# Transposing the running sums of the state space part once, and spreading each head's row with one product

## The reference, cut to what matters

```python
dt = softplus(dt_raw + dt_bias)                     # [tokens, heads]
a = -exp(a_log)
cum = cumsum(dt * a, axis=tokens)                   # [256, 32]
seg = cum[t, head] - cum[s, head]
decay_ts = exp(where(t >= s, seg, -inf))
w = (c_t . b_s) * decay_ts * dt_s
y[t] = sum over s of w[t, s] * x[s]                 # per head
```

## Time and profile before

| what | us |
|---|---|
| median of the runs (3) | 1957.97 |
| profiled execution, own time | 1953.04 |
| its span | 1951.2 |
| TensorE busy (PE) | 1786.4, 92% |
| VectorE busy (DVE) | 857.6, 44% |
| ScalarE busy (ACT) | 560.4, 29% |
| GpSimd busy (POOL) | 307.3, 16% |

### The profile page before, as it was taken

How to read it: one execution, slowest core, us unless ns; L and a number is a source line. 1 busy time by engine, 2 the same in 40 slices (tenths; PEclk the granted TensorE clock), 3 DMA queues, 4 the chain that set the end, 5 groups by cost and what they waited for, 6 DMA issues and landing times.

```text
span 1951.2 us, 32338 instructions
## 1 busy us (share of the span) xinstructions
PE 1786.4 (92%) x13254; PEld 1686.9 (86%) x13254; DVE 857.6 (44%) x2226; ACT 560.4 (29%) x1542; POOL 307.3 (16%) x284
## 2 busy tenths in 40 slices
PE   3999999999999878877899999997999999999998
PEld 2888887888889877777899899987999999899998
DVE  6631474333155677766968655333341113311010
ACT  1011224440033444434556432322322101321000
POOL 0100000000012544544334333230000000000000
PEclk9998999999999999999999999999999999999999
DMA  9952332133449999999999999996686687458883
GB/s 386 367 194 87 130 130 102 72 108 129 151 160 414 415 421 420 420 420 420 404 421 406 420 420 420 421 420 259 225 302 215 218 281 256 151 189 287 292 291 130
DMA packets 82658, 554.89 MB, mean 284 GB/s; under 512 B 8736, under 2 KB 15440, under 8 KB 15824
## 3 DMA queue, kind: packets, MB, share of 16 engines
q1 hardware_dynamic: 41088, 256.60, 36.2%
q0 software_dynamic: 39168, 285.23, 35.5%
q10 hardware_dynamic: 2256, 11.00, 1.4%
HBM read 551.72 MB, written 1.07 MB: 283 GB/s over the span
## 4 chain that ended last, share of the span: by engine, by line
PE 72%; DMA 17%; DVE 4%; ACT 3%; issue 3%; POOL 1%; ACTq 0%; DVEq 0%; POOLq 0%
PE PS L834 30%; PE PS L602 21%; PE PS L798 10%; DMA AUX<-in_peer_uv_dram,SCR 10%; DMA V<-in_peer_uv_dram,SCR 4%; DMA CONV<-in_peer_uv_dram,SCR 2%; PE PS L624 2%; PE PS L649 1%; DMA PROJ<-in_ada_dram 1%; DVE PROJ L1900 1%; PE PS L869 1%; PE PS L739 1%; PE PS L974 1%; PE PS L973 1%; PE PS L995 1%
## 5 line engine op out<-in xcount | busy, mean ns | idle before, releaser
L602 PE MATMUL PS<-H,ring 128*128 128x256 f32 x1408 | 314.9, 385 | 4.8 <-DVE H L1824 3.6
L602 PEld LDWEIGHTS PS<-H,ring 128*128 128x128 f32 x1408 | 270.3, 193 | 42.5 <-issue 4.3
L798 PE MATMUL PS<-PROJ,AUX 128*128 128x128 f32 x2048 | 254.3, 284 | 45.2 <-ACT PROJ L1283 45.0
L798 PEld LDWEIGHTS PS<-PROJ,AUX 128*128 128x128 f32 x2048 | 244.4, 199 | 52.7 <-ACT PROJ L1283 52.5
L834 PE MATMUL PS<-H,ring 128*128 128x128 f32 x2112 | 246.0, 275 | 0.0
L834 PEld LDWEIGHTS PS<-H,ring 128*128 128x128 f32 x2112 | 241.2, 192 | 1.0 <-issue 0.6
L1117 POOL DMA_INDIRECT AUX<-in_peer_uv_dram,SCR x128 | 145.5, 1137 | 552.7 <-DVE SCR L1884 314.2
L1900 DVE CUSTOM_DVE_ANT_0 PROJ<-AUX,PROJ 128x1024 f32<-128x1024 f32 x128 | 156.0, 1224 | 156.3 <-DMA AUX<-in_peer_uv_dram,SCR 155.9
L798 PE MATMUL PS<-PROJ,CONV 128*128 128x128 f32 x1536 | 187.6, 282 | 36.7 <-ACT PROJ L1283 36.7
L798 PEld LDWEIGHTS PS<-PROJ,CONV 128*128 128x128 f32 x1536 | 180.8, 197 | 41.6 <-ACT PROJ L1283 41.6
L834 PE MATMUL PS<-PROJ,ring 128*128 128x128 f32 x1632 | 187.9, 275 | 0.0
(11 more groups left out here) (299 smaller groups left out, 1772.4 us busy)
## 6 DMA issues: line engine op xcount, KB each, us to landing
ring<-in_stream_dram SPq DMA_DIRECT2D x181, 1024.0 KB, 4.9
AUX<-in_stream_dram SPq DMA_DIRECT2D x58, 1024.0 KB, 4.8
AUX<-in_ada_dram POOLq DMA_DIRECT2D x16, 1024.0 KB, 10.4
AUX<-in_ada_dram ACTq DMA_DIRECT2D x4, 1024.0 KB, 12.1
PROJ<-in_ada_dram ACTq DMA_DIRECT2D x4, 1024.0 KB, 21.0
AUX<-in_peer_uv_dram,SCR POOLq DMA_INDIRECT x128, 14.7
CONV<-bias_by_distance SPq DMA_DIRECT2D x1, 2048.0 KB, 12.6
CONV<-in_peer_uv_dram,SCR POOLq DMA_INDIRECT x96, 14.5
```

The lines of the kernel that those rows point to most:

```text
L602: mm = pe.matmul(acc(n, c), w[:, k, c * P:(c + 1) * P], src[:, g * DC + k, :], start=(g == 0 and k == 0 and (c == 0 or groups == 1)), stop ...
L798: mm = pe.matmul(y_chunk(t, c), UV[b][:, D + c * P:D + (c + 1) * P], DIAG[n % ND], start=(k == 0 and c % 4 == 0), stop=(k == SPT - 1), ski ...
```

## The change

A new job "ct" is put at h = 5: TensorE transposes `cum` (two transposes of 128 tokens by 32 heads) and VectorE copies the [32, 256] result to CUMT, on 32 partitions of `dts`, in the place of the four temporary fields. `cum_row(h)` then is one product: its stationary operand is column h of a 32 by 32 unit matrix, spread to 128 columns, its moving operand is CUMT.

```diff
@@ plan_jobs
         if h == 4:
             jobs += ["cum0", "cum1"]
+        if h == 5:
+            jobs.append("ct")
         if h:
             jobs.append(("yn", h - 1))
@@ program
         dt_, dtA, cum, dtx, dty, dtz, arow = (dts[:, i] for i in range(7))
+        CUMT = dts[0:32, 3:7].rearrange("p a t n -> p (a t n)")
@@ TensorE, loop over heads
+                if h == 5:
+                    o = open_bank(pe, "ct")
+                    for t in range(TT):
+                        wait_taken(pe, f"cum{t}")
+                        mm = pe.transpose(o[0:32, t * P:(t + 1) * P], cum[:, t, :], ident)
+                    made(mm, "ct")
                 if h:
                     norm_sum(h - 1)
@@ TensorE, cum_row
             def cum_row(h):
                 o = open_bank(pe, ("cr", h))
-                pe.matmul(o[:, 0:TOK], dtA[:, 0, h:h + 1].broadcast_to([P, P]), cst("triu"), start=True, stop=False)
-                made(pe.matmul(o[:, P:TOK], dtA[:, 1, h:h + 1].broadcast_to([P, P]), cst("triu", 0, P),
-                               start=False, stop=True), ("cr", h))
-
+                made(pe.matmul(o[:, 0:TOK], ident[0:32, h:h + 1].broadcast_to([32, P]), CUMT, start=True, stop=True), ("cr", h))
+
+            wait_taken(pe, "ct")
             for h in range(4):
                 cum_row(h)
@@ VectorE, loop over heads, behind head_var(h - 1)
+                if h == 5:
+                    wait_made(dve, "ct")
+                    taken(dve.tensor_copy(CUMT, bank("ct")[0:32, 0:TOK]), "ct")
```

## The result

The changed kernel takes 1965.79 us (median of 5, 1963.47 to 1969.34) against 1957.97 us: ratio 1.0041, 95% interval 1.0023 to 1.0059. A second set gave 1.0039 (1.0023 to 1.0054). By the means it is slower by 7.5 us in the first set and 7.6 us in the second; 0.8 us was forecast, too little to be told from nothing, and the time lies 4.2 us above the top of the range.

A forecast was written before the change was run, and what follows sets the result against it. TensorE, 72% of the chain, was taken to bound the kernel, with ScalarE and VectorE setting some places. Gains -3.3, changes of shape +1.4 and head 5 +2.7 gave +0.8 us: 1958.8 us, 8-in-10 range 1954.9 to 1961.6.

The forecast's parts named there:

- Gains from shorter rows: TensorE's rows, one product each: 0.22 us saved per head, 7.0 in all, of which 3.32 on the path.
- The rows in the middle of a block and behind the last `g` tile: Rows 10, 11, 14, 15, 18, 19, 22, 23 and 26 to 31: no gain, ScalarE and VectorE set the time.
- Changes of shape: Seven new changes on the path between 32-partition rows and full products: 0.2 us each, 1.4 us in all.
- The term of 0.6: Two transposes at head 5 with a change of shape in and out: 0.6 us, between 0.2 and 0.9.
- The wait at head 5: Second half of the scores waits for VectorE's copy behind a reciprocal: 2.7 us with the transposes, bounds 2.2 and 3.1.
- Sum of work: Whole kernel: gains -3.3, changes of shape +1.4 and head 5 +2.7 make +0.8 us.
- the rival "TensorE's clock falls": Heads 26 to 31, attention projection pays: +3.7 us, 1961.7; with a second fall at head 5, 1964.6; chance 0.08.
- the prediction's own last sign: TensorE's granted clock: the prediction fails if it leaves 1.00.
- cover for rows 4 and 5: Before the first `y` product TensorE idles 1.57 us for VectorE, so shortening rows 4 and 5 gives nothing.
- the idle 2.02 us at head 4 has 1.00: Argument against the clock falling: the stretch with that idle time at head 4 ran at 2.4 GHz throughout.
- fill a quarter of the array: Argument for the clock falling: heads 26 to 31 idle TensorE 0.22 us more each, rows using 32 of 128 partitions.

The follow-up runs named there:

- e3_rows_128: The change with VectorE's copy of the transposed sums ahead of head_var(4) and rows contracting over 128 partitions, not 32: -0.8 +- 2.0 us against before.
- e2: The change with VectorE's copy of the transposed sums moved ahead of head_var(4), rows still on 32 partitions: +4.1 +- 2.8 us against before.
- e1_ct_only: The change with the old two-product cum_row put back, keeping the transposes, copy and wait at head 5: +2.7 +- 2.5 us against before.
- e6: The change with its wait at head 5 kept, but rows contracting over all 128 partitions: +1.5 +- 2.0 us against before.
- e4_before_again: The kernel before, unedited, run again as a control with its own profile: -0.1 +- 1.9 us against before.
- e8_both_copies_first: e3_rows_128 with VectorE at head 4 also copying cum0 and cum1 ahead of head_var(3): -8.1 +- 2.2 us against before, ratio 0.9963, median 1949.99 us.
- e9: The kernel before with one edit, VectorE at head 4 copying cum0 and cum1 ahead of head_var(3): -1.0 +- 2.0 us against before.

## Why the prediction was wrong, point by point

**Gains from shorter rows: right.** From the last `cb` product to `g` tile 2 it is 2.84 us before, 2.23 in the profile after and 1.95 in e3_rows_128, where the full 0.88 show. Blocks are 11.40 us, 11.20 in e3. The rows in the middle of a block and behind the last `g` tile give nothing, as said: from `g` tile 7 to `attn` it is 18.34 us after and 18.23 before.

**Changes of shape: right for 32 partitions**, 0.2 us each: 11.40 against 11.20 for one, and for the two around rows 0 to 3 0.28 before tile 2 and 0.10 within it. **Wrong for the transposes:** with 32 columns between products of 128 they cost 0.22 us for both and nothing more (275.22 to 275.44 to the next product's normal start; head 5 in e2 is 2.69 against 2.47 us). The term of 0.6 was 0.2.

**The wait at head 5: right in place and making**, 2.5 us with the transposes where 2.7 stood; e1_ct_only has +2.7 +- 2.5, and taking the wait away saved 3.5 +- 3.9 (32 partitions) and 2.3 +- 3.0 us (128), which fits but is not clear of noise.

**Sum of work:** with these sizes -3.3 + 1.4 + 2.5 = +0.6 us. The measured change is 7.5. So the sum was sound and 7 us lay outside it. That the forecast's +0.8 is so near to +0.6 is in part luck: the transposes were put 0.4 too high and their wait 0.2 too low.

**The failed step is the rival "TensorE's clock falls", held at 0.08.** The sum of the forecast put the clock at nothing, and the prediction's own last sign, the granted clock leaving 1.00, is what came. The rival had one price, one place and one argument against it, and all three were off. The place: I put it at heads 26 to 31 and `attn`, where TensorE is least filled to the eye; there the clock stayed at 1.00 in the change's profile. It fell at pairs 0 and 1, where TensorE idles for ScalarE and VectorE (1.37 and 1.57 us before) and does thin work between, and where the earlier trace rows had shown that idle time to me as good news, cover for rows 4 and 5. The price: 2.9 us from one fall at head 2; here 5.5 in the stretch (85.96 us where the work gives 81.88 - 2.44 + 1.0 = 80.44), all but some 1.0 of it from the form on 32 partitions, and 1.7 in the profile behind head 5 (3.4 us at half the clock). 0.6 + 5.5 + 1.7 = 7.8, near the 7.5 measured. The runs bear out the 5.5 better than the 1.7: e1 and e6 lie 2.7 and 2.3 us above their partners, what the wait costs by work alone. The argument: "the idle 2.02 us at head 4 has 1.00" was one draw. In seven of eleven profiles the clock does fall behind that wait. The sentence that its rows "fill a quarter of the array" was the right lead; with 64 of 128 partitions the fall is short (one profile), with 32 it is long.

The Trainium skill, page "TensorE: Matmul & The Clock Gate", section "Part 1: The HAM clock gate", says that the gate follows how busy the array has been, and that how many slow matmuls one gets varies from run to run. The traces agree with the second: e4_before_again has falls at places where the first profile of before has none. They agree with the first in so far as the fall at the pairs begins in or right behind an idle time of 1.8 us on TensorE. e2 against e3 adds that after rows on 32 partitions the low clock lasts longer than after rows with as many columns on 128.

**Open.** Why e8_both_copies_first lies 8.1 us below before and not the 3 to 4 that its work allows (2.0 for head 4, 3.1 for rows without changes of shape, less 1 to 2 for the falls at the pairs); e3 and e9 alone have -0.8 and -1.0, and e8's mean granted clock, 0.9784, is hardly above the 0.9768 of before beside it. The falls that its profile lacks behind head 4 may be some of it, but e9 lacks them too. What it is in a product on 32 partitions that holds the clock less was not taken further; e3's weights are zero beyond one partition too, so it isn't how many of them are zero, but the data that stream through the other 96 partitions were not told apart from the number of partitions. The intervals against before are 2 to 3 us to a side, and each kernel but the two given ones has a single profile.

## What to carry to other kernels

Before a change takes work off TensorE, look where TensorE already waits: there the shorter work is no gain and the clock can fall, and the next full tiles pay for it. Contract over all 128 partitions with zeros in the unit column rather than over 32: it streams in the same time, needs no change of shape, and kept the fall of the clock short here. When a job is put into a rotation of banks, list the jobs four behind it, and put its reader ahead of any long instruction that doesn't need it; and price a fall of the clock at every place where the engine idles, not at one.

## What the runs showed of the hardware

A product on 32 partitions, 128 columns of weights and 256 columns of data in f32 takes 0.43 us like one on 128 (eight records, four products, from 338.83 to 340.75: 1.92 us, of which 0.2 is a change of shape). Each change between 128\*128 and 32\*128 costs 0.2 us, the ones around a product of 128\*32 nothing that shows. The clock fell while TensorE did short products between idle times of 1.4 and 1.8 us, and how long it stayed at 1.2 GHz went with the form of those products: 13.7 us with 32 partitions, 3.4 or 6.8 with 64 or 128. The mean clock of whole runs, 0.975 for the change and 0.977 to 0.979 for before, moves with their time: over the runs of before the correlation is -0.50, -0.61 and -0.68 in the three sets.
